# A hybrid decoder layer on one core: the output-projection stage put in another order, and attention probabilities divided in place

## What is computed

```python
x = x + 0.5 * rms_norm(swiglu(rms_norm(x, pre1)), post1)
P = rms_norm(x, pre_m) @ w_in          # q, k, v | hq, hf, hi, hg
A = sliding_window_attention(q, k, v)  # window 128, sinks, rotary; 8 q heads, 2 kv heads
H = hgrn2(hq, hf, hi)                  # 8 heads, chunked recurrence
H = rms_norm(H, out_g) * silu(hg)      # by head
x = x + rms_norm(concat(A, H) @ w_out, post_m)
x = x + 0.5 * rms_norm(swiglu(rms_norm(x, pre2)), post2)
```

```python
m = jnp.maximum(jnp.max(s, axis=-1, keepdims=True), sink)
p = jnp.exp(s - m)
denom = jnp.sum(p, axis=-1, keepdims=True) + jnp.exp(sink - m)
return p / denom
```

## Time and profile before

| what | value |
|---|---|
| three runs | 2202.56 us median (2198.28 to 2204.68) |
| the profiled execution's own time | 2196.1 us |
| its span, first to last instruction | 2194.3 us |
| busy: TensorE, VectorE, ScalarE, GpSimd | 95%, 53%, 26%, 15% |
| mean granted clock of TensorE | 0.979 of full |

### The profile page before, as it was taken

One profiled execution on the slowest core, in us unless ns is written; L12 is line 12 of the kernel. 1 busy time (PEld: TensorE's weight loads), 2 busy tenths in 40 slices (PEclk: granted clock), 3 DMA queues, 4 the chain that ended last, 5 costly groups with the idle time before them and its releaser, 6 DMA issues.

```text
span 2194.3 us, 33942 instructions
## 1 busy us (share of the span) xinstructions
PE 2086.3 (95%) x13727; PEld 2012.3 (92%) x13727; DVE 1152.5 (53%) x1861; ACT 563.1 (26%) x888; POOL 337.8 (15%) x158
## 2 busy tenths in 40 slices
PE   5999999999999989999999698899999999999996
PEld 5999999999999978988888587799999999999996
DVE  3554455544545485666665346754454544545446
ACT  4112111121111242244554534322111121111212
POOL 7111011110111133111110012321011110111100
PEclk9999999999999989999999889899999999999998
DMA  3111111111111112100010234111111111111111
GB/s 121 56 49 48 40 46 48 48 48 44 42 48 48 49 71 94 41 30 21 20 30 20 74 118 176 39 49 49 47 39 48 48 48 51 35 48 48 48 39 78
DMA packets 30776, 117.48 MB, mean 54 GB/s; under 512 B 4457, under 2 KB 5361, under 8 KB 28912
## 3 DMA queue, kind: packets, MB, share of 16 engines
q1 hardware_dynamic: 30704, 116.44, 16.6%
HBM read 105.61 MB, written 10.81 MB: 53 GB/s over the span
## 4 chain that ended last, share of the span: by engine, by line
PE 85%; DVE 8%; issue 2%; ACT 2%; DMA 1%; POOL 1%; SPq 0%; DVEq 0%; ACTq 0%; POOLq 0%
PE PS L370 24%; PE PS L371 24%; PE PS L372 24%; PE PS L502 2%; PE PS L503 2%; PE PS L504 2%; PE PS L548 2%; DVE h L1427 2%; DVE resid L1372 1%; PE PS L408 1%; PE PS L592 1%; DVE y L1367 1%; DMA o_raw<-in_w_out 1%; ACT sm L1155 1%; PE PS L579 1%
## 5 line engine op out<-in xcount | busy, mean ns | idle before, releaser
L370 PE MATMUL PS<-x_hi,w_hi 128*128 128x344 f32 x2480 | 803.3, 324 | 46.2 <-DVE w_lo L1354 22.5
L371 PE MATMUL PS<-x_lo,w_hi 128*128 128x344 f32 x2480 | 796.1, 321 | 0.0
L372 PE MATMUL PS<-x_hi,w_lo 128*128 128x344 f32 x2480 | 794.7, 320 | 0.0
L370 PEld LDWEIGHTS PS<-x_hi,w_hi 128*128 128x128 f32 x2480 | 470.6, 190 | 51.0 <-issue 27.6
L371 PEld LDWEIGHTS PS<-x_lo,w_hi 128*128 128x128 f32 x2480 | 470.5, 190 | 1.7 <-issue 0.2
L372 PEld LDWEIGHTS PS<-x_hi,w_lo 128*128 128x128 f32 x2480 | 470.2, 190 | 0.0
L808 POOL TENSOR_TENSOR raw<-raw,vecs 128x1024 f32<-128x1024 f32 x110 | 217.1, 1979 | 1373.0 <-DMA raw<-in_w_gu 1199.9
L1467 DVE TENSOR_TENSOR y<-y,PS 128x344 f32<-128x344 f32 x528 | 266.2, 511 | 187.9 <-PE PS L372 187.9
L370 PE MATMUL PS<-h,w_hi 128*128 128x344 f32 x1056 | 339.5, 321 | 7.0 <-DVE h L1427 6.2
L371 PE MATMUL PS<-h,w_hi 128*128 128x344 f32 x1056 | 337.6, 320 | 0.0
L372 PE MATMUL PS<-h,w_lo 128*128 128x344 f32 x1056 | 336.2, 318 | 0.0
(11 more groups left out here) (205 smaller groups left out, 1781.2 us busy)
## 6 DMA issues: line engine op xcount, KB each, us to landing
raw<-in_w_gu SPq DMA_DIRECT2D x88, 512.0 KB, 3.6
raw<-in_w_down SPq DMA_DIRECT2D x44, 512.0 KB, 3.5
raw<-in_w_in SPq DMA_DIRECT2D x22, 512.0 KB, 3.6
raw<-in_w_out SPq DMA_DIRECT2D x19, 512.0 KB, 3.8
resid<-in_x SPq DMA_DIRECT2D x3, 1376.0 KB, 9.1
stream_x<-resid SPq DMA_DIRECT2D x3, 1376.0 KB, 4.7
resid<-stream_x SPq DMA_DIRECT2D x3, 1376.0 KB, 6.6
out_y<-resid SPq DMA_DIRECT2D x3, 1376.0 KB, 4.7
```

The source lines that it names most:

```text
L370: nc.tensor.matmul(PS[:, bank, :GW], wh, vh, start=(k == 0), stop=False)
L371: nc.tensor.matmul(PS[:, bank, :GW], wh, vl, start=False, stop=False)
L372: mm = nc.tensor.matmul(PS[:, bank, :GW], wl, vh, start=False, stop=(k == last))
```

## The change

1. `probs_by_key` becomes a transpose: ScalarE divides the probabilities in place (`divide`), and TensorE turns them with the identity. `diag` goes.
2. The keys' cache arrives with rows of 128 elements, the last one zero, and is loaded whole.
3. In the last body `silu_gates(0)` comes before `probs(0)`, `hi_attention(0)` later, `hi_hgrn(0)` into the body, and `head_gated(0)` ahead of `states`.
4. Sample products are in another order: values after unit 2, outputs and scores after unit 3, attend after unit 7. `pick` has another place in memory.
5. Norm sums stand after other units. `border_low` and `border_fold` leave GpSimd and run whole on VectorE.
6. The last group is scaled, added and split in two halves of 4 tiles, and the first pair of FFN 2 waits for each half.

```diff
 # SP
-            sp.dma_start(k_win_s[:, :, 0:WINDOW - 1], ins["k_cache"]).then_inc(S["smp_in"], 16)
+            sp.dma_start(k_win_s[:], ins["k_cache"]).then_inc(S["smp_in"], 16)
...
 # PE, probs_by_key
-                    pe.wait_ge(S["diag_done"], 2 * i + h + 1)
+                    pe.wait_ge(S["divided"], 2 * i + h + 1)
...
-                            mm = nc.tensor.matmul(PS[:, 4 + q // 2, at_:at_ + CH], sm[:, h, q * w + a * CH:q * w + (a + 1) * CH],
-                                                  diag[:, q, :], start=True, stop=True)
+                            mm = nc.tensor.transpose(PS[:, 4 + q // 2, at_:at_ + CH], sm[:, h, q * w + a * CH:q * w + (a + 1) * CH], ident[:])
...
 # PE, output stage
-            out_units(2, 5)
-            sample_scores()
-            sample_outputs()
-            out_units(5, 6)
+            out_units(2, 3)
+            pe.wait_ge(S["croot_done"], 3)
+            sample_values()
+            out_units(3, 4)
+            pe.wait_ge(S["kv_done"], 1)
+            sample_outputs()
+            sample_scores()
+            out_units(4, 5)
...
-            sample_values()
-            out_units(9, 14)
-            pe.wait_ge(S["kv_done"], 1)
+            out_units(8, 12)
+            pe.wait_ge(S["s_attc_done"], 1)
             norm_sum(("F", 1, 0))
-            out_units(14, 18)
+            out_units(12, 17)
+            norm_sum(("S", 2, 0))
+            out_units(17, 18)
             norm_sum(("F", 1, 1))
-            out_units(18, 20)
-            norm_sum(("S", 2, 0))
-            out_units(20, OUT_TILES)
+            out_units(18, 23)
             norm_sum(("S", 2, 1))
+            out_units(23, OUT_TILES)
...
+            last_sum(0)
+            pe.wait_ge(S["x_split_lo_late"], NG * 2 + 1)
+            pair_unit(0, 0)
+            last_sum(1)
+            pair_unit(0, 1)
+            pe.wait_ge(S["x_split_lo_late"], NG * 2 + 2)
+            pair_unit(1, 0)
+            pair_unit(1, 1)
+            pair_unit(2, 0, halves=True)
+            norm_sum(("S", 2, 2))
+            pair_unit(2, 1)
...
 # ACT
-                def reciprocals(h):
+                def divide(h):
...
-                    if 2 * i + h:
-                        act.wait_ge(S["pt_done"], 2 * i + h)
                     for q in range(GQA):
-                        last = nc.scalar.activation(diag[:, q, :], ident[:], ACT.Copy, scale=rden[:, h, q:q + 1])
+                        part = sm[:, h, q * w:(q + 1) * w]
+                        last = nc.scalar.activation(part, part, ACT.Copy, scale=rden[:, h, q:q + 1])
...
 # POOL
-            border_low(0)
-            border_fold(0)
             gain(0, 41, V_GAIN["ffn2_pre"])
-            border_low(1)
             gain(1, 41, V_GAIN["ffn2_pre"])
-            border_fold(1)
...
 # DVE
             def border_low(g):
-                t = slice(POOL_TILES, KT)
                 dve.wait_ge(S["x_split_hi"], NG * 2 + g + 1)
-                nc.vector.tensor_tensor(x_lo[:, g, t], resid[:, g, t], x_hi[:, g, t].bitcast(F32), ALU.subtract)\
+                nc.vector.tensor_tensor(x_lo[:, g], resid[:, g], x_hi[:, g].bitcast(F32), ALU.subtract)\
                     .then_inc(S["x_split_lo_late"], 1)
...
+            def last_new(a):
...
+                t = half_of(a)
+                dve.wait_ge(S["rms_done"], norm_no[("F", 1, 2)] + 1)
...
-            ffn(G_FFN2, U_FFN2, 1, 2, lambda: None, {(0, 1): lambda: scaled(2), (1, 0): lambda: added(2), (1, 1): lambda: border_low(2)})
+            ffn(G_FFN2, U_FFN2, 1, 2, lambda: None, {(0, 0): last_halves, (0, 1): last_lows})
```

More of the change, by code:

```diff
@@ L319, in _ @@
             sp.dma_start(resid[:, 0], outs["x1"][0]).then_inc(resid_full[0], 16)
-            for k in range(7, 9):
-                load_out(k, 1)
+            load_out(7, 1)
             sp.wait_ge(S["vrow_done"], 1)
@@ L786, in by_then, with last_sum @@
-            def by_then(g):
-                if g == 0:
-                    norm_sum(("F", 1, 2))
-                elif g == 2:
-                    norm_sum(("S", 2, 2))
-            pair_by_group(G_FFN2, U_FFN2, x_ready, by_then)
+            out_units(23, OUT_TILES)
+            def last_sum(part):
+                i = norm_no[("F", 1, 2)]
+                pe.wait_ge(S["y2_folded"], part + 1)
+                if part == 0:
+                    pe.wait_ge(S["root_done"], i - 1)
+                for m in range(2):
+                    mm = nc.tensor.matmul(PS[:, 3 + i % 2, :GW], ones[:], sq_bufs[sq_no[("F", 1, 2)]][:, KT // 2 * part + m, :],
+                                          start=(part == 0 and m == 0), stop=(part == 1 and m == 1))
+                if part:
+                    mm.then_inc(S["ss_done"], 1)
@@ new lines, in pair_unit @@
+            def pair_unit(g, o, halves=False):
+                if g == 0:
+                    pe.wait_ge(S["w_ready"], READY_CREDIT + G_FFN2 + o + 1)
+                bank = (2 * g + o) % 3
+                pe.wait_ge(S["unit_evac"], U_FFN2 + 2 * g + o + 1)
+                for k in range(KT):
+                    if halves and k % (KT // 2) == 0:
+                        pe.wait_ge(S["x2_low"], 2 * k // KT + 1)
+                    wh, wl, vh, vl = w_hi[o][:, k * P:(k + 1) * P], w_lo[o][:, k * P:(k + 1) * P], x_hi[:, g, k, :], x_lo[:, g, k, :]
+                    nc.tensor.matmul(PS[:, bank, :GW], wh, vh, start=(k == 0), stop=False)
+                    nc.tensor.matmul(PS[:, bank, :GW], wh, vl, start=False, stop=False)
+                    mm = nc.tensor.matmul(PS[:, bank, :GW], wl, vh, start=False, stop=(k == KT - 1))
+                mm.then_inc(S["unit_done"], 1)
@@ L1752, in body @@
                     head_scaled(0)
+                    head_gated(0)
                 unit_end(3)
@@ L1756, in body @@
                     weights_low(3)
-                    head_gated(0)
                     return
@@ L1842, in _ @@
             nc.vector.tensor_scalar(p_s[0:64], p_s[0:64], st_s[0:64, 5:6], None, ALU.mult).then_inc(S["s_prob"], 1)
+            out_evac(6)
             out_split(9)
+            head_scaled(2)
             out_evac(7)
-            head_scaled(2)
             out_split(10)
+            head_gated(2)
             out_evac(8)
-            head_gated(2)
             out_split(11)
-            dve.wait_ge(S["kvp_done"], 1)
-            for t in range(TPH):
-                src = PS[:, 4:8, :].rearrange("p a (b t v) -> p t (a b) v", b=2, t=TPH)[:, t]
-                kvp = nc.vector.tensor_tensor(kv_s[:, t], src, kg_s[:, t, :].unsqueeze(2).broadcast_to([P, N_SAMPLE, HEAD]), ALU.mult)
-            kvp.then_inc(S["kv_done"], 1)
             out_evac(9)
+            low_hgrn(2)
             out_split(12)
@@ L1858, in _ @@
             out_split(13)
+            fold(("F", 1, 0))
             out_evac(11)
             out_split(14)
-            low_hgrn(2)
             out_evac(12)
+            scaled(0)
             out_split(15)
-            fold(("F", 1, 0))
             out_evac(13)
+            added(0)
             out_split(16)
```

189 lines of the change are left out of this document (114 added, 75 removed).

## The result

| | before | changed |
|---|---|---|
| median of 4 executions | 2200.42 us (2194.93 to 2204.68) | 2170.68 us (2169.21 to 2171.63) |
| profiled execution, its span | 2196.1, 2194.3 | 2169.2, 2167.4 |
| packets, under 512 bytes | 30776, 4457 | 29879, 3433 |

The changed kernel takes 0.9867 of the time, with a 95% interval of 0.9846 to 0.9888; the medians are 29.7 us apart. A second set of four executions beside nine of before gave 2170.54 us and 0.9868. The forecast of 2178.6 us was 8 us too high.

The account below looks back on a forecast made before the run. TensorE, busy 95% of the span, was taken as the bound: its own instructions in the bodies, waits and clock in the output stage. Savings 12.7 + 0.3 + 9.6 + 1.4 = 24.0 us take 2202.6 to 2178.6 us, range 2168 to 2193.

Parts of the forecast that it names:

- Bodies, 12.7 us: Probability groups in the bodies: eight transposes replace 16 matmuls, 0.91 us less per group, 12.7 us in all, bounds 9 and 14.
- The rival of a falling clock: At the 15 probability groups: the clock falls after each transpose group, making the kernel slower, 2230 us; chance 0.03.
- The stall: TensorE's 13.2 us wait before group 1's head sums: a 127-partition load on one DMA engine; it stays, growing to 17 or 18.
- a stall that shrinks: Sign of being wrong: the wait before the stage's first head sum shrinks; 16 to 19 us was expected.
- whatever TensorE gains in between: Between input projection's last unit and the stall's end: TensorE's gains only lengthen the stall, from 13 to 17 or 18 us.
- The walk through the waits: Output stage behind the stall: waits followed one by one, 13.6 us left against 23.2, a gain of 9.6 us.
- up to 1.4 us for each of two gains: Squares sum of group 1: GpSimd's two gains for FFN 2's weights slow VectorE; 5.6 us wait taken as 7.0.
- Clock, 1.4 us: Output stage: one fall of the clock less than before, some 1.4 us saved.
- the two sample groups stay: Output stage: the clock falls after the two groups of sample products, and two long waits, were claimed to remain.
- The slower one: Rival, 2230 us: 15 falls of the clock at probability groups, 3.4 us each, 51 us less 24; chance 0.03.
- the stall would go with the key rows: Rival, 2163 us: whole key rows end the 13.2 us wait and the slow head sum, 39.4 us less; chance 0.04.
- One half only: Rival, 2190 us: only the bodies' 12.7 us or only the stage's 11.3 us pays; chance 0.17.

Follow-up runs that it names:

- e1: The kernel before with only the probabilities divided in place and turned by transposes; 2189.7 us, ratio 0.9963.
- e10: The kernel before with probabilities divided in place and each of their transposes made twice into the same place; 2200.2 us, ratio 1.0000.
- e3: The changed kernel with the values' cache padded by a row so that its load covers 128 partitions, not 127; 2152.4 us, ratio 0.9796.
- e2: The changed kernel with the product by scaled identities put back in place of division and transposes; 2185.8 us, ratio 0.9942.
- e8: The changed kernel with low parts of 3 of 8 tiles and the fold back on GpSimd for groups 0 and 1; 2171.4 us, ratio 0.9871.
- after_again: The changed kernel as it is, executed once more as a second set; 2170.5 us, ratio 0.9868.
- e9: The changed kernel with the values' load on 128 partitions and the last body's order of before; 2159.7 us, ratio 0.9812.
- e7: The changed kernel with the values' load on 128 partitions and the first two sums of the stream's squares one unit later; 2147.2 us, ratio 0.9757.
- e6: The changed kernel with the first two sums of the stream's squares each one output unit later on TensorE; 2160.4 us, ratio 0.9827.
- e5: The kernel before with one edit, the values' load on 128 partitions; 2183.3 us, ratio 0.9929.

## Why the prediction was right, point by point

**Bodies, 12.7 us: right.** 0.91 us for a group, 1.9 us for a body, clock 1.00. The head sums of group 1 moved by 12.6 us, in e1 by 12.8, and e10, which puts equal work back, moved them back to 1262.3. That this meets 12.7 to 0.1 us is luck. The values' load is issued when the input projection ends; it stands at 1214.8 to 1218.5 us in the nine profiles with 8 transposes to a group, and at 1229.1 to 1231.6 in the four with 16 matmuls to a group, 13.9 us apart in the mean. The rival of a falling clock did not come about: the granted clock from 1050 to 1165 us is 1.00 in all of them, with groups of 0.9 us and, in e10, with groups twice as long. The Trainium skill's rule that transpose mode does not count as busy ("TensorE: Matmul & The Clock Gate", Part 4) does not show in groups this short between other matmuls; no run here has longer ones.

**The stall: right in kind, its size missed.** It is the values' load, shown by e3. The SyncE queue gives the fixed distance. In the kernel before:

```profile
1229.12 0.54 SPq L309 DMA_DIRECT2D v_win_s<-in_v_cache  x1
```

In the changed kernel:

```profile
1215.87 0.32 SPq L308 DMA_DIRECT2D v_win_s<-in_v_cache  x1
```

From here to the head sums it is 31.4 us before and 32.0 after, and between these two in the other seven kernels with the short load (e2 has it at 1230.54 and 1262.31). But the stall is 14.0 us (12.8 again), where I had 17 to 18. By the prediction's own sign of being wrong, a stall that shrinks, the two profiles stand on either side of the 13.2 us of before. The step that failed is "whatever TensorE gains in between": I let the whole 3.7 us of the issue wait, and the rest of the last body, count as gained. TensorE's timeline in the changed kernel shows what stayed:

```profile
1221.18 1.08 PE L601 MATMUL PS<-pT,v_tok 128*64 128x256 f32 x8 [1.20 <-ACT pT L1179]
1224.02 0.50 PE L367 MATMUL PS<-x_hi,w_hi 128*128 128x344 f32 x1 [1.75 <-issue]
...
1247.91 4.31 PE L509 MATMUL PS<-c_sq,head_ones 128*128 128x344 f32 x8 [13.99 <-ACT hv_s L1290]
```

1.75 us of it is left and 1.2 us of a new wait came in front; e1, with the old order, has 0.8 of that, so most of it comes with the transposes. Output unit 0 starts 8.2 us behind the load's issue, where it was 8.6. The clock during units 0 and 1 also counts in the stall: in e8 they run at 1.00 and it is 15.0 us, in after_again at 0.51 from 1225 to 1231 us and it is 12.8. It cost the forecast nothing, since the stall takes up any difference.

**The walk through the waits: right.** Forecast and measured: scores 0.5 and 0; first norm sum 0.9 and 0.9 (its terms add up to 8.5 us and not 8.4); squares of group 0 5.2 and 4.7; second norm sum 0 and 0; squares of group 1 7.0 and 8.3; last group 0 to 1 and 0. Together 13.6 and 13.9 us, a gain of 9.3 us against 9.6. Part of this is luck: two waits came out 0.5 us shorter each and one 1.3 us longer. The 1.3 us in group 1 are slower VectorE operations beside GpSimd's. VectorE's timeline of the changed kernel there, one row for the same low part in group 0, and GpSimd's two gains:

```profile
1331.07 3.02 DVE L1819 TENSOR_TENSOR x_lo<-resid,x_hi 128x2752 fp32r<-128x2752 f32 x1
...
1365.12 4.50 DVE L1819 TENSOR_TENSOR x_lo<-resid,x_hi 128x2752 fp32r<-128x2752 f32 x1
1369.55 2.91 DVE L1378 TENSOR_TENSOR w_lo<-raw,w_hi 128x1024 fp32r<-128x1024 f32 x1
1372.38 0.50 DVE L1802 COPY y<-PS 128x344 f32<-128x344 f32 x1
1372.81 1.57 DVE L1826 TENSOR_TENSOR sq_b<-sq_b 128x1376 f32<-128x1376 f32 x1
1364.85 1.90 POOL L833 TENSOR_TENSOR raw<-raw,vecs 128x1024 f32<-128x1024 f32 x1 [63.88 <-DMA raw<-in_w_gu]
1368.44 2.94 POOL L833 TENSOR_TENSOR raw<-raw,vecs 128x1024 f32<-128x1024 f32 x1 [1.70 <-DMA raw<-in_w_gu]
```

Beside them the low part grows by 1.5 us and the weight's split from 1.2 to 2.9. That is 3.2 us. The prediction names up to 1.4 us for each of two gains, but its 7.0 us hold only one of them (5.6 + 1.4); with both it would have said 8.4, and 8.3 was measured.

**Clock, 1.4 us: the term that was mis-sized.** It was 5.3 us in the profiled executions. I had "the two sample groups stay". But of their work the largest, the 128 outputs, ran at full clock: 3.90 us above. In the kernel before, and in e1 with the same old order, they took 6.99:

```profile
1271.06 6.99 PE L716 MATMUL PS<-qf,state_s 64*64 64x1 f32 x128
```

With the scores beside them the sample products took 9.2 us before and 6.5 after: 2.7 of the 3.9 us that I was off by. It is not the order alone. All four kernels with the old order have 6.99 us for the outputs; of the nine with the new one, six have 3.90 and three (e2, e3, e9) 5.4, with scores so much longer that these three are at 9.1 to 9.2 us again.

**Sum at the marks.** Forecast 12.7 + 0.3 + 9.6 + 1.4 = 24.0 us; measured 12.6 + 9.3 + 5.3 = 27.2. Medians fell by 29.7 us, 2.5 more, since the profiled execution of before was a quick one. The forecast also began from a median of three, 2202.6, which is 2.1 us above that of four.

**The rivals.** The slower one's price per fall was too high by its own rows: 25 matmuls in 6.70 us in place of 3.9 lose 2.8 us, not 3.4, which makes 2220 us of its 2230. None of its falls came. That the stall would go with the key rows: no, it goes with the 128th partition of the values, and 2152 us was the prize. One half only: each half pays alone, but the bodies' half alone returned 8 and not 12.7 us.

## What to carry to other kernels

Count the partitions of each load in front of a stall: one short of 128 left 508 KB to one DMA engine at 26 GB/s, some 20 us by these two numbers (an estimate, as the trace has no landing for it), where the full load landed in 6.9, and the output weight behind it was late. A padding row was worth more than half of this whole change. A walk of queue times over the waits of a stage was good to 1.3 us in one wait, and the waits that it left showed where to move a sum by one unit. What such a walk lacks is the clock, so test parts of a change together as well: alone they gave 21 us, together 29.

## What was not expected of the hardware

In a stage with waits the granted clock differed between kernels with the same 941 matmuls from 0.84 to 0.94, and their busy time from 155.3 us (e1) to 140.7 (e7). Removing a wait seemed to pay more than the wait: e6 took 6.8 us of waits away and gained 9.0, e3 took 14.0 and gained 15.8, e5 13.2 and 15.6. The three agree in direction, but each excess of about 2 us is within the intervals of the ratios. One kernel's executions can also stand in two groups 5 us apart (e5). What places the low spans was not found: starts 1.8 us apart and 23.2 us of waits each gave 172.1 us in one profile (before) and 176.3 in another (e10).

GpSimd's fold of the same size took 3.1 us twice in e8, and 3.5 and 4.07 us in the kernel before, with VectorE at work beside it each time; what makes the difference is not shown. The one duration that I took over, 4.07, overstated it by a third.
